# Results of an expert's unit written by ScalarE's DMA queue instead of GpSimd's

## The reference, cut to what matters

```python
def _hier_moe(m, ...):              # m: rmsnorm(h), (1024, 1024)
    # softmax over 4 groups, the best group; softmax over its 8 experts, the best two
    weights = g_w * e_w / sum(e_w)   # two weights per token
    experts = g_idx * 8 + e_idx      # two experts per token, of 32

def expert_block(tok, e):            # for the tokens that chose expert e
    xb = x_pad[tok]
    hb = silu(xb @ w_gate[e]) * (xb @ w_up[e])     # (., 1024) @ (1024, 512), twice
    return hb @ w_down[e]                          # (., 512) @ (512, 1024)
# y[token] += weight * row, for both experts of a token
```

## Time and profile before

| | |
|---|---|
| median of three timed runs | 3081.6 us (3078.67 to 3088.18) |
| profiled execution, its own time | 3090.64 us |
| its span in the profile | 3089.1 us |
| TensorE busy | 2816.6 us (91%) |
| VectorE busy | 1113.6 us (36%) |
| ScalarE busy | 650.4 us (21%) |
| GpSimd busy | 251.2 us (8%) |
| DMA | 609.37 MB, 197 GB/s over the span |

### The profile page before, as it was taken

The page is one execution under the profiler, slowest core; times in us unless marked ns, Lnnn a source line. Parts: engine busy times, 40 slices in busy tenths (PEclk is TensorE's granted clock), DMA queues, the critical chain, the costliest instruction groups (busy, mean ns, idle before and its releaser), DMA issues. The chain is left out here.

```text
span 3089.1 us, 40774 instructions
## 1 busy us (share of the span) xinstructions
PE 2816.6 (91%) x16517; PEld 1452.0 (47%) x16518; DVE 1113.6 (36%) x2450; ACT 650.4 (21%) x1254; POOL 251.2 (8%) x376
## 2 busy tenths in 40 slices
PE   7999999999898889888989999877998989898798
PEld 4544555555632222224467744477655323222343
DVE  2585355544400000005464635566463000000152
ACT  3310355531100000003321123422211100000130
POOL 0000000001100000002000000044211000000110
PEclk9999999999899999999999899988998999999999
DMA  4000692031699999976020120000417999999731
GB/s 160 28 28 0 273 408 82 1 114 60 251 365 391 402 395 395 389 314 230 34 66 1 16 70 28 1 2 2 173 68 284 371 398 397 398 398 401 317 140 41
DMA packets 137045, 609.37 MB, mean 197 GB/s; under 512 B 25700, under 2 KB 32260, under 8 KB 120456
## 3 DMA queue, kind: packets, MB, share of 16 engines
q1 hardware_dynamic: 111848, 529.08, 44.4%
q0 software_dynamic: 21632, 74.46, 6.6%
q10 hardware_dynamic: 3376, 3.19, 0.3%
HBM read 503.80 MB, written 101.71 MB: 196 GB/s over the span
## 5 line engine op out<-in xcount | busy, mean ns | idle before, releaser
L1990 PE MATMUL acc<-wg,xt 128*128 128x512 f32 x512 | 224.1, 599 | 0.0
L2644 PE MATMUL acc<-xt,work 128*128 128x512 f32 x384 | 166.9, 593 | 0.0
L672 PE MATMUL acc<-h,xt 128*128 128x512 f32 x384 | 165.2, 592 | 0.0
L1990 PEld LDWEIGHTS acc<-wg,xt 128*128 128x128 f32 x512 | 98.0, 193 | 120.5 <-issue 120.5
L1709 PE MATMUL py<-place 128*32 128x512 f32 (+2 forms) x608 | 131.3, 639 | 17.7 <-issue 15.7
L310 PE MATMUL scores<-qkt 65*128 65x512 f32 (+7 forms) x384 | 146.0, 489 | 0.4 <-DVE qkt L451 0.4
L1709 PE MATMUL pu<-place 128*32 128x512 f32 (+2 forms) x768 | 140.2, 624 | 0.0
L1709 PE MATMUL pg<-place 128*32 128x512 f32 (+2 forms) x736 | 137.7, 594 | 0.2 <-issue 0.2
L457 DVE TENSOR_REDUCE nmax<-scores 128x1 f32<-128x256 f32 (+7 forms) x128 | 96.8, 756 | 73.9 <-PE scores L312 70.3
L672 PEld LDWEIGHTS acc<-h,xt 128*128 128x128 f32 x384 | 72.9, 190 | 91.1 <-issue 90.9
L1220 PE MATMUL acc<-place 128*128 128x512 f32 x256 | 112.7, 594 | 1.1 <-PEq L71 1.1
(11 more groups left out here) (648 smaller groups left out, 5295.6 us busy)
## 6 DMA issues: line engine op xcount, KB each, us to landing
place<-in_moe_w_gate_dram SPq DMA_DIRECT2D x21, 2048.0 KB, 24.9
own<-in_moe_w_gate_dram SPq DMA_DIRECT2D x20, 2048.0 KB, 23.7
place<-in_moe_w_up_dram SPq DMA_DIRECT2D x20, 2048.0 KB, 26.9
slots_out<-zeros SPq DMA_DIRECT2D x4, 9216.0 KB, 63.0
place<-in_moe_w_down_dram SPq DMA_DIRECT2D x18, 2048.0 KB, 26.5
own<-in_moe_w_down_dram SPq DMA_DIRECT2D x18, 2048.0 KB, 27.5
own<-in_moe_w_up_dram SPq DMA_DIRECT2D x14, 2048.0 KB, 24.7
xt<-in_moe_w_down_dram SPq DMA_DIRECT2D x10, 2048.0 KB, 29.5
```

Source lines behind the costliest of these rows:

```text
L672: last = pe.matmul(acc[:, n % 4, 0:width], xs[:, k, tile_of(i)], weights[:, k, cols], start=(k == 0), stop=(k == k_of - 1))
L1990: last = pe.matmul(acc[:, u % 4, :], xt[:, k, i * P:(i + 1) * P], wg[:, k, n * SLAB:(n + 1) * SLAB], start=(k == 0), stop=(k == KD - 1))
L2644: last = pe.matmul(acc[:, n % 4, :], slabs[m // 4 % 2][:, k, (m % 4) * P:(m % 4 + 1) * P], xt[:, k, half * SLAB:(half + 1) * SLAB], start= ...
```

## The change

GpSimd's loop in `first_blocks` keeps only the input rows. The issues of the result rows of units 0 to 19 go into ScalarE's program: in pass n, behind the copy of unit n+1's turned rows, ScalarE waits for its own and for VectorE's half of unit n-1 and issues that unit's rows. It now loads the expert numbers that it needs itself. The result rows of unit 20 stay with SyncE. The semaphores `y_out` count as before, and GpSimd still waits for the last two of them at the end.

```diff
@@ GpSimd
-                def rows_out(n):
-                    pool.wait_ge(y_act, n + 1)
-                    pool.wait_ge(y_dve, n + 1)
-                    for x in units[n]:
-                        pool.dma_start(c.slots_out[bass.ds(expert[x.q] * P + x.slot, x.rows), :], y[x.row:x.row + x.rows, n % 2]).then_inc(y_out[n % 2], 16)
-
-                for n in range(UNITS):
-                    if n + 2 < UNITS:
-                        pool.wait_ge(x_turned, n + 1)
-                        rows_in(n + 2)
-                    if n:
-                        rows_out(n - 1)
+                for n in range(UNITS - 2):
+                    pool.wait_ge(x_turned, n + 1)
+                    rows_in(n + 2)
                 for n in (UNITS - 3, UNITS - 2):
                     pool.wait_ge(y_out[n % 2], y_before[n % 2] + 16 * arrivals[n])
@@ ScalarE
+                expert = {q: q for q in range(FIXED)}
+
+                def rows_out(n):
+                    act.wait_ge(y_act, n + 1)
+                    act.wait_ge(y_dve, n + 1)
+                    for x in units[n]:
+                        if x.q not in expert:
+                            expert[x.q] = act.value_load(r.table[0:1, 3, x.q:x.q + 1], min_val=0, max_val=EXPERTS - 1)
+                        act.dma_start(c.slots_out[bass.ds(expert[x.q] * P + x.slot, x.rows), :], y[x.row:x.row + x.rows, n % 2]).then_inc(y_out[n % 2], 16)
...
                     if n:
                         y_half(n - 1)
                     if n + 1 < UNITS:
                         turned_out(n + 1)
+                    if n:
+                        rows_out(n - 1)
                 y_half(UNITS - 1)
```

## The result

| | before | after |
|---|---|---|
| median of five timed runs | 3081.6 us (3076.8 to 3088.2) | 3056.2 us (3053.8 to 3065.9) |
| ratio of the times | | 0.9925, 95% interval 0.9903 to 0.9947 |
| profiled execution (span) | 3090.6 us (3089.1) | 3055.4 us (3053.7) |
| silu of the first to that of the last unit, layer 1 | 512.3 us | 493.7 us |
| the same, layer 2 | 506.0 us | 495.2 us |

A forecast was written before the change was run, and what follows sets the result against it. The prediction took the experts' stages to be paced by DMA bandwidth, with TensorE 3 us a unit behind. Its terms, 0 + 0 + 0 + 0, left the timed median at 3081 us, range 3068 to 3096.

The forecast's parts named there:

- Removed from GpSimd: Experts' stages: 38 issues a layer, 19.4 us, leave GpSimd, and rows in go up to 2.2 us sooner; worth 0.
- Added to ScalarE: Each unit: waits, register loads and issues hold ScalarE 1.3 to 5.6 us, taken as 2.8.
- What hides it: Each unit: ScalarE's idle time and TensorE's room cover holds up to 26.5 us, so the cost is 0.
- The hold: ScalarE's issues: standing behind a long SyncE pair would hold it 18.8 us, still under 26.5; time unmoved.
- End of the stage: Last units' result rows: unit 19's are down by 1378, ahead of the last unit's; 0.
- Moved between queues: Rows out of units 0 to 19, 10.5 MB a layer, change queue: at most 8.4 us saved in all, taken as 0.
- the rival on three queues: Just after each turn, rows out, rows in and weights share the rate; weights land later, 24 us slower, 3105; chance 0.09.
- Three queues instead of two: Just after each turn, three transfers at once delay the weights 0.67 us; 36 units pay 24 us, 3105; chance 0.09.
- Cheaper rows: Rows out become as cheap as weights in ScalarE's queue: up to 8.4 us faster, 3073; chance 0.16.
- ScalarE held too long: Two long holds in one unit, 32.0 us, exceed the cover by 5.5: at most 39 us slower, 3120; chance 0.06.
- The sign that I named for a wrong forecast: Experts' stages: both steady windows, 513 and 506 us, change by over 5 us each in the same direction.

The follow-up runs named there:

- both_act: The changed kernel with the rows in also issued by ScalarE, behind the rows out, so GpSimd's queue carries no rows there: 3085.3 us, 0.9994 of before.
- apart_one: The kernel before, but GpSimd issues rows in first and holds rows out until the up products are done: 3082.7 us, 0.9981 of before.
- in_sp: The changed kernel with the rows in issued by SyncE, in the weights' queue between two weight tiles: 3136.3 us, 1.0158 of before.
- gathered_before: The kernel before, but each unit's rows in come as one indirect DMA of 128 rows from an interleaved table: 3036.8 us, 0.9853 of before.
- whole_before: The kernel before, but each unit's rows in are one DMA of 128 partitions, the second expert's rows being wrong: 3042.1 us, 0.9853 of before.
- serial_two: The changed kernel, but GpSimd waits for the last rows out to land before issuing the next rows in: 3102.5 us, 1.0050 of before.
- apart_two: The changed kernel, but ScalarE holds the rows out until the up products are done: 3076.6 us, 0.9957 of before.
- swap: The changed kernel with the engines exchanged, rows in issued by ScalarE and rows out by GpSimd: 3055.5 us, 0.9919 of before.

## Why the prediction was wrong

**What held.** The analysis that DMA paces the stage: each kernel's stage followed its rate, and TensorE did the same matmuls in it. *Removed from GpSimd*, worth 0: both_act empties GpSimd and gains nothing. Its wait simply moved to the rows in (409.5 us, against the 402.9 of the earlier trace rows). *Added to ScalarE*: two issues with their register loads took 0.81 to 1.78 us, half of them less than my lower bound of 1.3; I had taken 2.8. *What hides it*: at the last unit ScalarE still idled 13.87 us before the silu:

```profile
844.54 0.60 ACT L1774 ACTIVATE place<-pg 128x512 f32<-128x512 f32 x1 [8.78 <-PE pg L1700]
...
1338.20 0.60 ACT L1774 ACTIVATE place<-pg 128x512 f32<-128x512 f32 x1 [13.87 <-PE pg L1700]
```

*The hold*: none. The longest of ScalarE's issues was 0.563 us. A SyncE issue of the commonest form took up to 4.3 us in the same stages:

```profile
L1657 SPq DMA_DIRECT2D place<-in_moe_w_gate_dram x20: 337/338/4292, 832.4 to 1307.8; - x20
```

If the lock wait of the Trainium skill (Perfetto Trace Analysis, "DMA Instruction — HWDGE (DVE, Sync)") is what lengthens SyncE's issues, it hardly reached ScalarE: over its shortest issue, 0.321 us, the longest has 0.24 more. I had also read the earlier trace rows wrongly: a row with x2 in the timeline spans the time between its two instructions, a wait for a free weight tile included. The source view of before has the single issues, the longest of them 7.0 us, so even the holds of my rival were too long. *End of the stage*, 0: the last two transfers stand as before, the last one by SyncE.

```profile
1346.67 0.81 ACTq L1767 DMA_DIRECT2D slots_out<-place  x2
1367.93 1.28 SPq L1664 DMA_DIRECT2D slots_out<-place  x2
```

**The step that failed** is *Moved between queues*: "at one end the rows stay as dear as they are; at the other they become as cheap as the weights", 8.4 us at most, of which I took 0. It priced the rows by their own engine time and took the weights' as fixed; the rival on three queues says why, "since the bytes are the same". In the runs the price of the weights moved, from 40.6 to 39.1 engine-us per MB. For 147.68 MB that is 1.5 x 147.68 / 16 = 14 us of the window's 400, the larger part of its gain. In these runs the engines' time per MB went with what moved at the moment and not with the queue: while a unit's rows came in, all transfers together ran at 283 GB/s instead of 425. The row I had (9.0 us of landing for rows in, 7.0 for rows out) did point at the rows in; I concluded "which stay", and so no change, without asking whether something can fill the time that they spoil. The cause of the overlap even stands in the prediction, under *Removed from GpSimd*: rows in issued up to 2.2 us sooner. I put it at 0 because the rows are wanted 50 us later, and didn't ask what they would then move beside.

**The rivals.** *Three queues instead of two* described the event rightly (rows out and rows in at once, just after the turn) and had the sign wrong. It shared out a constant 393 GB/s; but the rate over the first nine microseconds of a burst rose from a mean of 353 to 380, and from 1 to 10 us behind a turn the weights moved no less than before (2.46 MB before, 2.51 after), so they didn't lose. `pg` waited 1.9 us in all where it had waited 0.6, which may be the mechanism that it named; the price was about one microsecond, not 24. *Cheaper rows* came nearest in sign for a cause that both_act denies: there the rows took 12.0% in a hardware queue. By the guess of the Trainium skill that two engines run slower because software rings share their ports (DMA: Bandwidth & Descriptors, "Latency and other measured facts"), both_act, whose software queue carries no rows, should have gained at least what after did; it gained nothing. The traces don't part the sixteen engines, so whether two of them are slower isn't seen. *ScalarE held too long* did not occur. The sign that I named for a wrong forecast, both steady stretches off by over 5 us in one direction, appeared: 18.7 and 10.8.

**What stays open.** Shown: reads of a unit's rows from DRAM to SBUF in pieces of fewer than 128 rows lower the rate of all traffic, in the queues of GpSimd (apart_one), ScalarE (both_act) and SyncE (in_sp); one piece of 128 hardly does (gathered_before, whole_before). Not shown: why. The runs change the number of pieces and the partitions that a piece fills together, so they don't tell whether each further DMA costs, or whether a piece on 96, 64 or 32 partitions loads the sixteen engines unevenly. The rows out, in the same pieces, cause no dip of their own (apart_one), so the direction matters; that favours neither. Open too are how the gain divides between the overlap and the sooner rows in, why rows out moved at the same time fill the dip only in part, and how much the size of the weights' packets beside the rows counts.

## What to carry to other kernels

Where a stage is bound by DMA at a share of 1.0, read the GB/s beside it, and look for the moments at which it falls: a share of 1.0 says that the engines are occupied, not that they are used well. Before moving a transfer to another queue, ask what it will then move beside, and what each transfer alone does to the rate. Here, bringing the rows in as one DMA of 128 partitions gave 47 us, and letting other traffic move beside the pieces gave 25. A price per byte averaged over a window can't be carried over to a change that shifts what overlaps.

## What the runs showed of the hardware

- Reads in pieces of 96 and 32 rows of 4 KB with nothing else of the rows beside them, among loads of 2 MB: all transfers together fall to 265 to 309 GB/s for some 3 us (before, both_act, apart_one), against some 425 without them; with a gather of 128 scattered rows they stay at 383 or more.
- The same reads later in a unit, beside weights in packets of 16 KB: 301 to 339 GB/s for eight microseconds, and a median of 11.3 us from issue to landing instead of 8.2 (serial_two, apart_two).
- A gather of 128 rows by an indirect DMA in the software queue is as good as a direct DMA of the same shape: 3036.8 us against 3042.1. GpSimd spends 0.99 us on one, and it landed in 9.4 us.
- Software and hardware queues cost nearly the same here: in after rows in took 5.6% for 8.06 MB in q0 and rows out 5.2% for 7.89 MB in q10; exchanged, in swap, 5.5% for 7.99 MB in q10 and 5.5% for 8.01 MB in q0. The times of the two kernels are equal (3056.2 and 3055.5 us).
